# A bidirectional mixer rebuilt inside a two-model kernel: seven products for its forget blocks, logarithms of the keys, paired states

## The reference, cut to what matters

```python
def hgrn2_chunk_scan(q, k, log_f, v, s0):        # chunks of 64 tokens, 8 heads of 128
    def step(state, inp):
        qc, kc, gc, vc = inp
        L = jnp.cumsum(gc, axis=2)
        o_inter = jnp.einsum('bhtk,bhkv->bhtv', qc * jnp.exp(L), state)
        diff = L[:, :, :, None, :] - L[:, :, None, :, :]
        decay = jnp.where(mask, jnp.exp(jnp.where(mask, diff, 0.0)), 0.0)
        a = jnp.einsum('bhtk,bhtsk,bhsk->bhts', qc, decay, kc)
        o_intra = jnp.einsum('bhts,bhsv->bhtv', a, vc)
        L_end = L[:, :, -1:, :]
        new_state = jnp.exp(L_end[:, :, 0, :])[..., None] * state + jnp.einsum(
            'bhsk,bhsv->bhkv', kc * jnp.exp(L_end - L), vc)
        return new_state, o_inter + o_intra

def gates(z):                                     # log forget, key
    f = lb + (1.0 - lb) * jax.nn.sigmoid(z)
    return heads(jnp.log(f)), heads(1.0 - f)
```

## Time and profile before

| | |
|---|---|
| three executions | 3176.93 to 3181.07 us, median 3180.95 |
| the profiled execution | 3184.92 us, its span 3183.1 |
| mean granted clock of TensorE | 0.984 of full speed |
| TensorE busy | 3013.5 us (95%) |
| VectorE busy | 1760.8 us (55%) |
| ScalarE busy | 683.4 us (21%) |

### The profile page before, as it was taken

How to read it: one execution, slowest core, us unless ns; L and a number is a source line. 1 busy time by engine, 2 the same in 40 slices (tenths; PEclk the granted TensorE clock), 3 DMA queues, 4 the chain that set the end, 5 groups by cost and what they waited for, 6 DMA issues and landing times. The chain is left out here.

```text
span 3183.1 us, 52421 instructions
## 1 busy us (share of the span) xinstructions
PE 3013.5 (95%) x22638; PEld 2345.8 (74%) x22638; DVE 1760.8 (55%) x2612; ACT 683.4 (21%) x1310; POOL 40.7 (1%) x80
## 2 busy tenths in 40 slices
PE   8999988999999999999899999989999999988998
PEld 8987764559976998674467995555888885555897
DVE  5554555556555564555456566584334663196665
ACT  1102113112112101212212103271111002144210
POOL 1000000000001000000000000000000000000000
PEclk9999999999999999999999999999999999999999
DMA  8645312227646746323216744201222442231442
GB/s 277 220 170 183 132 48 101 80 80 231 212 159 211 245 171 208 132 68 107 80 54 218 246 150 149 80 1 53 80 96 89 146 166 92 80 106 60 159 159 106
DMA packets 279638, 430.34 MB, mean 135 GB/s; under 512 B 9944, under 2 KB 147520, under 8 KB 279408
## 3 DMA queue, kind: packets, MB, share of 16 engines
q1 hardware_dynamic: 273920, 411.52, 38.1%
q0 software_dynamic: 5024, 14.34, 1.4%
q10 hardware_dynamic: 464, 1.12, 0.1%
HBM read 425.91 MB, written 1.05 MB: 134 GB/s over the span
## 5 line engine op out<-in xcount | busy, mean ns | idle before, releaser
L455 PE MATMUL bank<-xT,ring 128*128 128x128 f32 (+3 forms) x4608 | 787.0, 330 | 10.5 <-DVE arena L825 5.7
L455 PE MATMUL bank<-arena 64*64 64x64 f32 (+9 forms) x7244 | 732.9, 283 | 47.6 <-DVEq L4032 8.5
L455 PEld LDWEIGHTS bank<-xT,ring 128*128 128x128 f32 (+1 forms) x4608 | 676.7, 192 | 113.7 <-issue 54.8
L455 PEld LDWEIGHTS bank<-arena 128*128 128x128 f32 (+4 forms) x7244 | 632.9, 163 | 146.6 <-issue 31.5
L455 PE MATMUL bank<-ring,xT 128*128 128x512 f32 (+2 forms) x1536 | 578.9, 549 | 7.7 <-DMA ring<-in_ple_w_gate 3.5
L455 PE MATMUL bank<-ring,arena 128*128 128x256 f32 (+1 forms) x1584 | 447.3, 435 | 17.7 <-DVE arena L882 6.5
L455 PEld LDWEIGHTS bank<-ring,xT 128*128 128x128 f32 (+1 forms) x1536 | 257.0, 183 | 271.5 <-issue 252.4
L455 PEld LDWEIGHTS bank<-ring,arena 128*128 128x128 f32 x1584 | 302.0, 193 | 135.2 <-issue 87.3
L825 DVE TENSOR_TENSOR arena<-arena,bank 128x256 f32<-128x256 f32 (+1 forms) x198 | 92.2, 466 | 399.3 <-PE bank L455 259.8
L736 ACT COPY arena<-bank 128x256 f32<-128x256 f32 (+1 forms) x264 | 107.8, 408 | 749.5 <-PE bank L455 748.0
L785 DVE TENSOR_TENSOR arena<-ring,arena 128x1024 f32<-128x1024 f32 (+1 forms) x216 | 257.1, 1190 | 7.4
(11 more groups left out here) (391 smaller groups left out, 2104.6 us busy)
## 6 DMA issues: line engine op xcount, KB each, us to landing
ring<-in_ffn_w SPq DMA_DIRECT2D x88, 1024.0 KB, 8.0
ring<-in_w_in SPq DMA_DIRECT2D x32, 2048.0 KB, 7.8
ring<-in_ffn_w_in SPq DMA_DIRECT2D x44, 1024.0 KB, 6.8
arena<-in_ada_w SPq DMA_DIRECT2D x20, 2048.0 KB, 13.4
ring<-in_ffn_w SPq DMA_DIRECT2D x16, 2048.0 KB, 8.0
ring<-in_ffn_w_out SPq DMA_DIRECT2D x12, 2048.0 KB, 8.0
ring<-in_hgrn_w_in SPq DMA_DIRECT2D x12, 2048.0 KB, 7.8
ring<-in_ffn_w SPq DMA_DIRECT2D x8, 1536.0 KB, 6.8
```

What stands on the lines that cost most here:

```text
L455: return self.e.matmul(o, lhsT, rhs, start=start, stop=stop, skip_group_check=True)
```

## The change

The mixer:

- Three forget blocks (the second forward one, both backward ones) are multiplied by seven products of 256 columns, 56 matmuls a block, from banks of the `to_dve` ring. VectorE makes the sums of weights (`dve_forget_T`) and of inputs (`dve_forget_x`), ScalarE keeps four banks' contents, VectorE adds, ScalarE takes the sigmoids from SBUF.
- In the levels VectorE subtracts half by half: the prefix sum for queries, prefix sum minus key logarithm for keys. ScalarE's exponential then gives the decayed key at once, written to its place after the scoring before it; VectorE multiplies only queries. Two logarithms of keys are new (`log_keys`).
- The backward prefix sums are made from the forward scan, shifted by one token.
- After the levels: keys need no multiplication; the products inside chunks come before the states; forward and backward states are multiplied in pairs; each step's states are read between the steps; the norm's weights go into the gates ahead, and the squares are summed by halves.

Elsewhere:

- `release` also hangs on transposes (`pe_turn_x`, `pe_norm_mod`, `pe_norm_tile`).
- At the start the identity is loaded alone and first, `x` in two halves, the other constants after `x`, layer-norm weights after the second weight block; the condition vectors are turned after the first feed-forward block. ScalarE's first activation table is loaded by a small copy.
- At the end the last product is joined before the residual is applied; GpSimd weights the left half of the columns, ScalarE scales it, VectorE does the right half, and each half of the tokens is stored by itself.

The diff, cut to what the text speaks of:

```diff
+                        if k == 0:
+                            pe.release(mm)
...
@@ -894,9 +912,15 @@
                 apply(s, half % 2, 0, w.sum[:, 0].rearrange("p (a n) -> p a n", a=2), True)
                 dve.wait_ge(down_products, 7 * h + 6)
                 add(w.sum[:, 1, 0:256], w.u, acc[4])
-                apply(s, half % 2, 1, w.sum[:, 1].rearrange("p (a n) -> p a n", a=2), False)
-                dve.wait_ge(down_products, 7 * h + 7)
-                apply(s, half % 2, 1, acc[7].unsqueeze(1).broadcast_to([P, 2, 256]), True)
+                rows1, last_product = w.sum[:, 1].rearrange("p (a n) -> p a n", a=2), acc[7].unsqueeze(1).broadcast_to([P, 2, 256])
+                if join_last and half == last:
+                    dve.wait_ge(down_products, 7 * h + 7)
+                    add(rows1, last_product, rows1)
+                    apply(s, half % 2, 1, rows1, True)
+                else:
+                    apply(s, half % 2, 1, rows1, False)
+                    dve.wait_ge(down_products, 7 * h + 7)
+                    apply(s, half % 2, 1, last_product, True)
...
+            act.e.dma_start(cst[:, 0:P], a["cst"][:, 0:P]).then_inc(ident_landed, 16)
+            for tt, landed in enumerate((x_landed, second_x_landed)):
+                act.e.dma_start(xtok[:, tt], a["x"][0, tt * P:(tt + 1) * P, :]).then_inc(landed, 16)
...
+                chain = (chain0, chain1)[b % 2]
+                B = forget_parts(pe.block())
+                T1, T2, T4 = forget_T_views(g)
+                product(chain, B[0][0], A[0][0], True, True)
+                if b:
+                    pe.wait_ge(combined, 4 * n)
+                product(single, B[1][0], A[0][1], True)
+                pe.wait_ge(T_sums, 4 * (T0 + g) + 1)
+                if first == 0:
+                    pe.wait_ge(x_sums, X0 + 2)
+                product(pair, T1, S1, True)
+                pe.wait_ge(products_kept, 4 * n + 1)
+                pe.wait_ge(T_sums, 4 * (T0 + g) + 2)
+                product(chain, T2, S2)
+                pe.wait_ge(combined, 4 * n + 1)
+                pe.wait_ge(T_sums, 4 * (T0 + g) + 3)
+                product(single, T4, A[1][1], True)
+                pe.wait_ge(products_kept, 4 * n + 2)
+                pe.wait_ge(x_sums, X0 + (2 if first else 4))
+                product(pair, B[1][1], S4)
+                pe.wait_ge(products_kept, 4 * n + 3)
+                pe.wait_ge(T_sums, 4 * (T0 + g) + 4)
+                product(chain, B[0][1], S3)
+                pe.used()
...
+                n = FIRST_FORGET + first + i
+                chains, single, pair = forget_banks[back]
+                chain = chains[i % 2]
+                dve.wait_ge(products, 7 * n + 2)
+                dve.wait_ge(products_kept, 4 * n + 1)
+                combine(b, 0, f_kept[:, 0], single[:])
+                if i + 1 < len(blocks):
+                    dve_forget_T(dve, first + i + 1)
+                dve.wait_ge(products, 7 * n + 6)
+                dve.wait_ge(products_kept, 4 * n + 3)
+                combine(b, 2, f_kept[:, 2], pair[:])
+                dve.wait_ge(products, 7 * n + 7)
+                dve.wait_ge(products_kept, 4 * n + 4)
+                combine(b, 1, f_kept[:, 3], chain[:])
+                combine(b, 3, f_kept[:, 1], chain[:])
...
@@ -3709,13 +3888,16 @@
                 if u % 2:
                     pe.used()
 
-            forget(stream_by_stream)
+            stream_by_stream(pe.block())
+            pe.used()
+            pe_gate_rows(pe, (0,), hdiag)
+            pe_forget7(pe, 0, 1)
             for _ in range(2):
                 blk = pe.block()
                 pe_tok(pe, blk, to_act, 0, 512, x_lhs, (2, 3))
                 pe.used()
             first_state(0, hv_ctx)
-            forget()
+            pe_forget7(pe, 1, 2)
             for _ in range(2):
                 blk = pe.block()
...
+            def state_products(i):
+
+                for b in range(2):
+                    pair = []
+                    for _ in range(2):
                         pe.wait_ge(to_dve.freed, to_dve.next_free())
-                        bank = to_dve.free_bank()
-                        for j in range(4):
-                            s_ = slice((4 * b + j) * P, (4 * b + j + 1) * P)
-                            mm = pe.mm(bank[:, j * P:(j + 1) * P], hkend_tok[back][r_, tt, s_], hv[r_, tt, s_])
+                        pair.append(to_dve.free_bank())
+                    for j in range(4):
+                        s_ = slice((4 * b + j) * P, (4 * b + j + 1) * P)
+                        for back, bank in enumerate(pair):
...
+            def read_states(i):
+
+                for b in range(2):
+                    for j in range(4):
+                        h = 4 * b + j
+                        for back in (1, 0):
+                            n = 3 - i if back else i
+                            q0 = h * SEQ + n * C
+                            mm = pe.mm(readout_banks[n // 2, b][CHUNKS[n % 2], j * P:(j + 1) * P], hF[back][:, q0:q0 + C],
+                                       hS[back][i][:, h], False, i == 3)
+                            if i == 3 and j == 3:
+                                mm.then_inc(to_act.filled, 1)
+
+            pe.wait_ge(key_tok_ready, pe.due(key_tok_ready, 2))
+            state_products(0)
+            state_products(1)
+            pe.wait_ge(queries_decayed, pe.due(queries_decayed))
+            read_states(0)
             pe.wait_ge(state_ready, pe.due(state_ready))
-            for tt in range(2):
-                for b in range(2):
-                    bank = readout[tt][b]
-                    for back in range(2):
-                        for j in range(4):
-                            h = 4 * b + j
-                            for c in range(2):
-                                n = 2 * tt + c
-                                q0 = h * SEQ + n * C
-                                mm = pe.mm(bank[64 * c:64 * c + 64, j * P:(j + 1) * P], hF[back][:, q0:q0 + C],
-                                           hS[back][3 - n if back else n][:, h], False, back == 1)
-                    mm.then_inc(to_act.filled, 1)
+            read_states(1)
+            state_products(2)
+            pe.wait_ge(state_ready, pe.due(state_ready))
+            read_states(2)
+            pe.wait_ge(state_ready, pe.due(state_ready))
+            read_states(3)
 
...
+            def decay(back, h, half):
+                diff = bw_diff_ready if back else diff_ready
+                part = halves(hF[back], h, not back)[half]
+                dst = halves(hK, h, not back)[1] if half else part
+                act.wait_ge(diff, act.due(diff))
+                ins = e.activation(dst, part, ACT.Exp, scale=-1.0 if half else 1.0)
+                ins.then_inc(decay_ready, act.up(decay_ready))
                 act.wait_ge(decay_ready, act.sent(decay_ready))
 
             for l, h in enumerate(LEVELS):
-                decay(1, h, 0, bw_diff_ready, act.due(bw_diff_ready))
-                decay(0, h, 1, diff_ready, act.due(diff_ready))
+                decay(1, h, 0)
+                decay(0, h, 0)
                 late_unit(l)
+                act.wait_ge(to_dve.filled, level_scored[l])
+                decay(1, h, 1)
+                decay(0, h, 1)
...
-                                     border.broadcast_to([P, n, 2 * h]), ALU.subtract)
+            src = (hb, hk)[half][back]
+            out_, in_ = halves(hF[back], h, not back)[half], halves(src, h, not back)[half]
+            return eng.tensor_tensor(out_, in_, border.broadcast_to([P, KT * SEQ // (2 * h), h]), ALU.subtract)
...
@@ -4024,14 +4256,13 @@
             for l, h in enumerate(LEVELS):
                 for back in (1, 0):
                     dve.wait_ge(decay_ready, dve.due(decay_ready))
-                    for i, (dst, src) in enumerate(((hQ, hq), (hK, hk[back]))):
-                        step(v.tensor_tensor(halves(dst, h, not back)[i], halves(src, h, not back)[i],
-                                             halves(hF[back], h, not back)[i], ALU.mult))
-                    if back and h != LEVELS[-1]:
-                        diff(1, LEVELS[l + 1])
+                    step(v.tensor_tensor(halves(hQ, h, not back)[0], halves(hq, h, not back)[0],
+                                         halves(hF[back], h, not back)[0], ALU.mult))
+                dve.wait_ge(decay_ready, dve.due(decay_ready, 2))
                 dve.sem_inc(level_ready, dve.up(level_ready))
                 if h != LEVELS[-1]:
-                    diff(0, LEVELS[l + 1])
+                    for back in (1, 0):
+                        diff(back, LEVELS[l + 1])
                 for tt in range(2):
                     dve.wait_ge(to_dve.filled, to_dve.next_filled())
...
+            dve_rstd(dve, tt, FINAL_SCALE[tt], scale_ready)
+            x = xtok[:, tt, 512:D]
+            ins = nc.vector.scalar_tensor_tensor(out=x, in0=x, scalar=FINAL_SCALE[tt], in1=lnp[:, 1, 512:D],
```

(9 more changed lines are left out.)

428 lines of the change are left out of this document (291 added, 137 removed).

## The result

The changed kernel took 3145.69 us, median of four runs (3143.25 to 3148.42). The kernel before stood at 3181.01 (3176.93 to 3181.58). The ratio is 0.9892, 95% interval 0.9875 to 0.9909: 35 us faster, where 35 were forecast. The profiled execution has a span of 3146.6 us, 36.5 less than the 3183.1 of before. The sum came out right; of its terms one is off by half, and something that the prediction didn't have makes up for it. That shows only when the span is cut at places that both kernels have.

A forecast was written before the change was run, and what follows sets the result against it. TensorE was taken as the bound, busy 3013.5 of 3183.1 us. Terms of -5.0, -3.5, -8.0, -10.2, -5.3 and -3.3 sum to -35.3 us, taking the median 3180.95 to 3146; range 3137 to 3160.

The forecast's parts named there:

- Start: Kernel start: with identity and `x` loaded before other constants, the first product comes at 12.6 instead of 17.61; -5.0 us.
- weights that come at their own pace: Kernel start: the first weight block is no faster without the constants, first product stays near 17; +5, 3151 us; chance 12%.
- Gate: Gate projection: releasing blocks on transposes removes TensorE's whole 3.5 us wait for the second gate load; -3.5 us.
- Forget blocks: Three forget blocks: seven products cut each from 27.50 to 24.17 us, less 2 us of waits for banks; -8.0 us.
- seven products in series: Forget blocks: each product waits for its bank's ScalarE and VectorE chain, blocks take 27 us again; +8, 3154 us; chance 10%.
- Levels: Levels' stretch: VectorE's work falls from 11.05 to 8.95 us a level, under TensorE's 9.08, ending the waits; -10.2 us.
- States and readout: From the last late unit to the output's turn: less work behind the third state, 8.6 us instead of 13.3; -5.3 us.
- The bound of -2: Chunk states and readout: smallest gain, if VectorE's new decay of queries, 2.3 us, falls in the chain; -2 us.
- rival on TensorE's clock: State stretch: more gaps drop the granted clock for two or three more groups; +4 to +8, 3153 us; chance 15%.
- Pairs: State products: alternating forward and backward could cut a step's 32 records from 3.5 to 2.0 us; counted as nothing.
- End: Kernel end: split final scaling and half-size last store; issue 2.1 us earlier, store 1.2 us shorter; -3.3 us.
- rival on the throttle: Whole kernel: TensorE, idling 35 us less, is throttled; a mean clock of 0.970 gives 3189 us; chance 3%.

## Why the prediction was right, point by point

- **Start, -5.0; measured -5.4.** The load order and the conditions each hold the first product if put back. The rival, weights that come at their own pace, fell. The identity loaded first, `x` in halves and the early table load weren't put back, so their share (the first turn stands at 7.74 in place of 10.35) isn't known. The product moved by 4.9, and its first records were 1.0 faster, which the sum didn't have. And 12.6, so near to 12.75, was partly luck, because the working misread. The 1.12 MB there are ScalarE's queue, that is `x` itself; GpSimd's queue with the constants is this row, by 16 us in the kernel before:

```profile
q0 software_dynamic: 432, 1.94, 31.2%
```

So 5.05 MB had moved by 16 us and not 4.1, and the same proportion gives 9.8 us in place of 12.1. It also took the loads to run evenly from the span's start; in the changed kernel 3.70 MB had moved by 12.75. What was misread and what was left out nearly cancel.

- **Gate, -3.5; measured -3.6.** The wait of 3.4 came back when the early release was taken out; the 2.8 us of lower clock behind it weren't in the working, nor in the kernel before.
- **Forget blocks, -8.0; measured -7.65**, with the two short waits (0.85 each, which cost 1.0 each from start to start, as forecast) and the cover for VectorE's sums. The rival, seven products in series, fell: no wait inside a block.
- **Levels, -10.2; measured -10.4.** The slow spell of the fifth level went with the waits, and came back with two added instructions, though not with one. The working had VectorE at 8.95 us a level, just under TensorE; it takes 9.23, just over. The levels are free of waits because VectorE starts 3.6 us ahead and six levels use up only 0.15 each. With some more levels, the sum would have been wrong.
- **States and readout, -5.3; measured -2.7. This is the step that failed in size.** The term "I let the third state come where it came, 25 us after the late unit" was mis-sized: it came 27.4 us after it. The part behind it, 8.6, was 8.8. The bound of -2 named VectorE's decay of queries; the runs show another cause for most of it: readings at the low clock ahead of the products that VectorE needs next (1.8 us of 2.6 went when the order was turned). The executions with the readings at full clock take 34.5 to 34.8 us without any edit, which is 1.0 to 1.3 us above the 33.5 forecast: with one more instruction in the levels the third state comes after 25.7 us and the part behind it takes 8.8. So the clock is worth 1.7 us of the 2.6, and the last 1 us lies mostly ahead of the third state, without a cause shown. The rival on TensorE's clock was right here in part, with 1.7 us at the readings and not the 4 to 8 it named; behind the output's turn the clock fell too, but it had before, so it cost nothing new.
- **Pairs, nothing in the sum.** Rightly so: alternating forward and backward gives TensorE 0.5 us per 16 records, and the stretch doesn't feel it.
- **End, -3.3; measured -2.9** against before, 3.3 when put back. The last store is issued 1.6 us nearer to TensorE's last product (2.1 forecast) and the span ends 1.3 us sooner after it (1.2 forecast).
- **The total.** The 2.7 us that the terms lack and the 3.9 of the stretches where nothing changed cancel for the most part: 32.6 + 3.9 is 36.5. The mean granted clock of the profiled execution is 0.986, against 0.984, so the rival on the throttle fell. In the two stretches of recurrent branches (235.83 to 710.11, 1212.44 to 1686.52 before) the profiled execution of before took 474.3 and 474.1 us, the changed one 472.6 and 469.0. The executions of the experiments, with the same code there except for the release in one, took between 468.1 and 472.7 in the first and between 469.1 and 474.0 in the second. So some 5 us in each depend on the execution, and that 35.3 was hit so exactly is partly luck. The experiment without early releases took 468.1 us in the first, so they aren't the cause there. Only one execution of before was profiled, and whether it was an unlucky one isn't settled. The range's upper end, 3160, lay below the 3163 that the terms' own ends give; that didn't matter here.

## What to carry to other kernels

Once an engine that fed the bound one no longer makes it wait, compare its work per round with the round itself: here VectorE runs 0.15 us over and lives on a lead of 3.6 us, so an added instruction costs nothing in the first levels and then most of its time (6.2 us of added work cost 3.9). In a chain between two engines, put the work that the other engine waits for ahead of the work that nobody waits for, above all where the clock may be low. A forecast whose total is right can still have a wrong term: cut both traces at common places before believing it.

## What the runs showed of the hardware

Seven matmuls whose result nobody uses, put in a wait of 6.1 us, kept TensorE's granted clock at 1.00 where it otherwise fell to 0.50 (0.66 on average over the ten us), and saved 1.6 us in the 16 records behind it (8.73 to 7.13) and 0.9 in the turn ahead of them (1.97 to 1.09).

The same code at the same place had its readings at full clock in three executions (65 records in 4.02 us) and partly at the lower in five (5.49 to 5.98); what decides that between executions no run here shows.

Records of 64 rows took 1.16 us for 16 when they alternated between the two halves of TensorE's rows, and 1.68 us when eight of one half stood ahead of eight of the other.
